# A two-block transformer kernel on one core: the tiles of SBUF laid out in another order, and the rows of x scaled before they are turned

## Time and profile before

| | |
|---|---|
| three runs, us | 1514.72, 1513.34, 1510.06; median 1513.34 |
| the profiled execution, us | 1509.91 |
| its span, first to last instruction, us | 1508.2 |
| PE busy | 1462.3 us (97%), 6907 matmuls |
| PE's weight loads busy | 1177.3 us (78%) |
| DVE, ACT, POOL busy | 789.5, 577.0, 102.6 us |

### The profile page before, as it was taken

One profiled execution on the slowest core, in us unless ns is written; L12 is line 12 of the kernel. 1 busy time (PEld: TensorE's weight loads), 2 busy tenths in 40 slices (PEclk: granted clock), 3 DMA queues, 4 the chain that ended last, 5 costly groups with the idle time before them and its releaser, 6 DMA issues.

```text
span 1508.2 us, 20254 instructions
## 1 busy us (share of the span) xinstructions
PE 1462.3 (97%) x6907; PEld 1177.3 (78%) x6907; DVE 789.5 (52%) x1232; ACT 577.0 (38%) x949; POOL 102.6 (7%) x83
## 2 busy tenths in 40 slices
PE   6999999899899999999999999999999999999997
PEld 5788877677867888888888777787787887878885
DVE  4538888775456544254445574344444344345552
ACT  5434444434545442124333353333333333333232
POOL 0000000101303000000033220000000000000001
PEclk9999999999999999999999999999999999999999
DMA  4322213223412333323323232221222312213231
GB/s 145 86 70 69 73 45 92 70 81 115 140 42 84 86 97 96 110 75 95 110 84 93 60 105 61 79 87 56 87 72 67 91 42 87 87 56 98 86 97 70
DMA packets 242783, 126.16 MB, mean 84 GB/s; under 512 B 17026, under 2 KB 241363, under 8 KB 242738
## 3 DMA queue, kind: packets, MB, share of 16 engines
q1 hardware_dynamic: 242162, 123.47, 28.3%
q10 hardware_dynamic: 576, 2.10, 0.4%
HBM read 123.45 MB, written 2.10 MB: 83 GB/s over the span
## 4 chain that ended last, share of the span: by engine, by line
PE 70%; issue 17%; DVE 4%; POOL 4%; ACT 2%; DMA 2%; SPq 0%; POOLq 0%; DVEq 0%; ACTq 0%
PE lin L556 20%; PE lin L560 19%; PE lin L559 19%; PE sc L633 3%; PE ob L647 3%; PE tr L641 1%; DVE wl L1394 1%; POOL kt L531 1%; ACT wh L1026 1%; POOL logit L538 1%; POOL qt L531 1%; PE tr L598 1%; PE sc L693 1%; DMA raw<-in_w_xkv_dram 1%; PE sc L598 1%
## 5 line engine op out<-in xcount | busy, mean ns | idle before, releaser
L1394 DVE TENSOR_TENSOR wl<-raw,wh 128x1024 fp32r<-128x1024 f32 x238 | 292.1, 1237 | 189.7 <-ACT wh L1026 185.2
L556 PE MATMUL lin<-uh,wh 128*128 128x512 f32 x752 | 304.2, 404 | 4.6 <-DVE pt L1867 2.0
L560 PE MATMUL lin<-uh,wl 128*128 128x512 f32 x752 | 294.1, 391 | 0.0
L559 PE MATMUL lin<-ul,wh 128*128 128x512 f32 x752 | 293.7, 390 | 0.0
L1026 ACT ACTIVATE wh<-raw 128x1024 fp32r<-128x1024 f32 x238 | 239.0, 1012 | 130.8 <-DMA raw<-in_w_mlp_dram 42.4
L556 PE MATMUL lin<-vh,wh 128*128 128x512 f32 x576 | 238.8, 415 | 1.7 <-DVE pt L1867 0.9
L559 PE MATMUL lin<-vl,wh 128*128 128x512 f32 x576 | 227.4, 395 | 0.0
L560 PE MATMUL lin<-vh,wl 128*128 128x512 f32 x576 | 227.3, 395 | 0.0
L556 PEld LDWEIGHTS lin<-uh,wh 128*128 128x128 f32 x752 | 141.7, 188 | 39.0 <-issue 4.6
L559 PEld LDWEIGHTS lin<-ul,wh 128*128 128x128 f32 x752 | 141.8, 189 | 29.8 <-issue 2.6
L560 PEld LDWEIGHTS lin<-uh,wl 128*128 128x128 f32 x752 | 141.5, 188 | 30.3
(11 more groups left out here) (356 smaller groups left out, 1721.1 us busy)
## 6 DMA issues: line engine op xcount, KB each, us to landing
raw<-in_w_in_dram SPq DMA_DIRECT2D x101, 512.0 KB, 3.6
raw<-in_w_mlp_dram SPq DMA_DIRECT2D x64, 512.0 KB, 4.0
raw<-in_w_out_dram SPq DMA_DIRECT2D x16, 512.0 KB, 3.5
raw<-in_w_xkv_dram SPq DMA_DIRECT2D x8, 512.0 KB, 3.5
raw<-in_w_proj_b_dram SPq DMA_DIRECT2D x8, 512.0 KB, 3.5
raw<-in_w_proj_a_dram SPq DMA_DIRECT2D x8, 512.0 KB, 3.5
xtok<-in_x_dram ACTq DMA_DIRECT2D x4, 512.0 KB, 5.1
raw<-in_w_mla_out_dram SPq DMA_DIRECT2D x4, 512.0 KB, 3.8
```

Source lines behind the costliest of these rows:

```text
L556: ins = pe.matmul(o, wh[:, slot, at], xh_, start=start, stop=False)
L559: pe.matmul(o, wh[:, slot, at], xl_, start=False, stop=False)
L560: return pe.matmul(o, wl[:, slot, at], xh_, start=False, stop=stop)
L1394: dve.tensor_tensor(wl[:, c.slot(4), 0:size], raw[:, c.slot(2), 0:size], wh[:, c.slot(4), 0:size].bitcast(F32), ALU.subtract).then_inc(lo_ ...
```

## The change

It has three parts. (1) The declarations of SBUF tiles are put in another order. From the bottom: `uh` 0 to 16 KB, `ul` 16 to 32; then the phase tiles, which share 32 to 96 KB: `vh` 32 to 48 and `vl` 48 to 64, `fh` 32 to 64 and `fl` 64 to 96, `cqh`, `cql`, `ckh`, `ckl` in 32 to 52, `yh`, `yl`, `oh`, `ol` in 32 to 64, `xuh`, `xul` in 32 to 64, `memh`, `meml` in 72 to 88, `xoh`, `xol` in 80 to 96, `gates`, `xtok`, `xn`, `av`, `gb` in 64 to 96; above them `wh` 96 to 112, `wl` 112 to 128, `raw` 128 to 136, `h` 136 to 152, then the tables and work tiles, `acc`, `ya` and the rest up to 207.3 KB. (2) A new tile `xn` holds x's rows times `rstd`. ACT takes the square root for each quarter by itself, that of quarter q - 1 behind the squares of quarter q; DVE takes its reciprocal and scales the 128x1024 quarter. PE waits for the four scaled quarters, and `turn_normed` is now a transpose, four of 128x128 for each tile. The diagonal tiles and `x_diag` go. (3) Two small DVE steps (`both`, `hb`) stand behind `lower(Idx(1))` in place of ahead of `norm_rstd("mix")`.

```diff
-        h = sb("h", [P, DT, S])
         uh = sb("uh", [P, DT, S], F32R)
         ul = sb("ul", [P, DT, S], F32R)
-        raw = sb("raw", [P, 2, 1024])
+
+        st = ExitStack()
+        cqh = sb("cqh", [P, 3, S], F32R, st)
...
+        st = ExitStack()
+        vh = sb("vh", [P, DT, S], F32R, st)
+        vl = sb("vl", [P, DT, S], F32R, st)
+        av = sb("av", [P, PAIRS, S], stack=st)
+        gb = sb("gb", [P, PAIRS, S], stack=st)
+        st.close()
+        fh = sb("fh", [P, 16, S], F32R)
+        fl = sb("fl", [P, 16, S], F32R)
         wh = sb("wh", [P, 4, 1024], F32R)
         wl = sb("wl", [P, 4, 1024], F32R)
+        raw = sb("raw", [P, 2, 1024])
+        h = sb("h", [P, DT, S])
...
@@ PE
-                for q in range(QT):
-                    ins = pe.matmul(sc[f % 3][:, q * P:(q + 1) * P], xtok[:, q, f * P:(f + 1) * P],
-                                    te[:, q * P:(q + 1) * P], start=True, stop=True)
-                ins.then_inc(xt_ready, 1)
+                turn_tile(sc[f % 3], lambda q: xn[:, q, f * P:(f + 1) * P]).then_inc(xt_ready, 1)
...
-            pe.wait_ge(x_diag, 1)
+            pe.wait_ge(xn_made, QT)
...
@@ ACT
+            def x_deviation(q):
+                act.wait_ge(xsq_made, q + 1)
+                act.activation(std[:, q:q + 1], x_sq[:, q:q + 1], ACT.Sqrt, bias=eps, scale=1.0 / D)\
+                    .then_inc(x_std if q < QT - 1 else std_made, 1)
+
             for q in range(QT):
                 act.wait_ge(x_landed[q], 16)
+                wait(act, xsq_made, q)
                 act.activation(logit[:, 0:D], xtok[:, q, :], ACT.Square, accum_out=x_sq[:, q:q + 1]).then_inc(xsq_made, 1)
-                act.wait_ge(xsq_made, q + 1)
-            act.activation(std, x_sq, ACT.Sqrt, bias=eps, scale=1.0 / D).then_inc(std_made, 1)
+                if q:
+                    x_deviation(q - 1)
+            x_deviation(QT - 1)
...
@@ DVE
+            def x_normed(q):
+                if q < QT - 1:
+                    dve.wait_ge(x_std, q + 1)
+                    dve.reciprocal(rstd[:, q:q + 1], std[:, q:q + 1]).then_inc(x_rstd, 1)
+                    dve.wait_ge(x_rstd, q + 1)
+                else:
...
+                dve.wait_ge(x_landed[q], 16)
+                dve.tensor_scalar(xn[:, q, :], xtok[:, q, :], rstd[:, q:q + 1], None, ALU.mult).then_inc(xn_made, 1)
+
+            x_normed(0)
+            x_normed(1)
             dve.wait_ge(vec_ready, 1)
             dve.tensor_copy(cols[:], tr[0][:, 0:NVEC]).then_inc(vec_copied, 1)
+            x_normed(2)
+            x_normed(3)
             dve.wait_ge(vec_copied, 1)
-            step(dve.tensor_tensor(both[:], cols[:, COL["final_norm_g"]:COL["final_norm_g"] + DT],
-                                   cols[:, COL["g_norm_2"]:COL["g_norm_2"] + DT], ALU.mult))
-            step(dve.tensor_scalar(hb, cols[:, COL["conv_ln_b"]:COL["conv_ln_b"] + CT], 0.5, None, ALU.mult))
-            norm_rstd("mix")
-            for q in range(QT):
-                ins = dve.tensor_scalar(te[:, q * P:(q + 1) * P], ident[:], rstd[:, q:q + 1], None, ALU.mult)
-            ins.then_inc(x_diag, 1)
             lower(Idx(0))
             for f in range(DT):
                 dve.wait_ge(xt_ready, f + 1)
                 gain_low(ul[:, f, :], sc[f % 3][:], col("norm_mix_g", f), uh[:, f, :], f + 1)
             lower(Idx(1))
+            step(dve.tensor_tensor(both[:], cols[:, COL["final_norm_g"]:COL["final_norm_g"] + DT],
+                                   cols[:, COL["g_norm_2"]:COL["g_norm_2"] + DT], ALU.mult))
+            step(dve.tensor_scalar(hb, cols[:, COL["conv_ln_b"]:COL["conv_ln_b"] + CT], 0.5, None, ALU.mult))
```

More of the change, by code:

```diff
@@ L164, in build @@
         ob = bank("ob")
-        h = sb("h", [P, DT, S])
         uh = sb("uh", [P, DT, S], F32R)
         ul = sb("ul", [P, DT, S], F32R)
-        raw = sb("raw", [P, 2, 1024])
+        st = ExitStack()
+        cqh = sb("cqh", [P, 3, S], F32R, st)
+        cql = sb("cql", [P, 3, S], F32R, st)
+        ckh = sb("ckh", [P, 2, S], F32R, st)
+        ckl = sb("ckl", [P, 2, S], F32R, st)
+        z = sb("z", [P, CT, S + PAD], stack=st)
+        st.close()
+        st = ExitStack()
+        yh = sb("yh", [P, CT, S], F32R, st)
+        yl = sb("yl", [P, CT, S], F32R, st)
+        oh = sb("oh", [P, 4, S], F32R, st)
+        ol = sb("ol", [P, 4, S], F32R, st)
+        s2 = ExitStack()
+        xtok = sb("xtok", [P, QT, D], stack=s2)
+        xn = sb("xn", [P, QT, D], stack=s2)
+        s2.close()
+        gates = sb("gates", [P, 16, S], stack=st)
+        st.close()
+        st = ExitStack()
+        xuh = sb("xuh", [P, DT, S], F32R, st)
+        xul = sb("xul", [P, DT, S], F32R, st)
+        s2 = ExitStack()
+        memtok = sb("memtok", [P, 2, D], stack=s2)
+        memh = sb("memh", [P, DT, MEM], F32R, s2)
+        meml = sb("meml", [P, DT, MEM], F32R, s2)
+        s2.close()
+        xp = sb("xp", [P, 2, QT, MEM], stack=st)
+        xpt = sb("xpt", [P, 2, 2, S], stack=st)
+        xoh = sb("xoh", [P, XH, S], F32R, st)
+        xol = sb("xol", [P, XH, S], F32R, st)
+        st.close()
+        st = ExitStack()
+        vh = sb("vh", [P, DT, S], F32R, st)
+        vl = sb("vl", [P, DT, S], F32R, st)
+        av = sb("av", [P, PAIRS, S], stack=st)
+        gb = sb("gb", [P, PAIRS, S], stack=st)
+        st.close()
+        fh = sb("fh", [P, 16, S], F32R)
+        fl = sb("fl", [P, 16, S], F32R)
         wh = sb("wh", [P, 4, 1024], F32R)
         wl = sb("wl", [P, 4, 1024], F32R)
+        raw = sb("raw", [P, 2, 1024])
+        h = sb("h", [P, DT, S])
         ident = sb("ident", [P, P])
@@ L204, in build @@
         st = ExitStack()
-        gates = sb("gates", [P, 16, S], stack=st)
         acc = sb("acc", [P, CT, S], stack=st)
         otok = sb("otok", [P, QT, S], stack=st)
[L208 to L218, removed]
         st.close()
         st = ExitStack()
-        xtok = sb("xtok", [P, QT, D], stack=st)
         vrows = sb("vrows", [P, P], stack=st)
@@ L226, in build @@
         xq = sb("xq", [P, XH, S], stack=st)
[L227 to L237, removed]
         xk = sb("xk", [P, XH, MEM], stack=st)
@@ L240, in build @@
         st.close()
[L241 to L250, removed]
-        ybh, ybl = uh, ul
[L252 to L256, removed]
+        ya = sb("ya", [P, PAIRS, S])
+        ybh, ybl = uh, ul
+        otp = sb("otp", [P, QT, P])
+        rbc = sb("rbc", [P, S])
+        nlog = sb("nlog", [P, S])
+        atok = sb("atok", [P, QT, P])
         cq = gates[:, 11:16, :]
@@ L274, in build @@
         x_landed = [sem(f"x{q}_landed") for q in range(QT)]
-        xsq_made, x_diag, x_turned = sem("xsq_made"), sem("x_diag_made"), sem("x_turned")
+        xsq_made, x_turned = sem("xsq_made"), sem("x_turned")
+        x_std, x_rstd, xn_made = sem("x_std"), sem("x_rstd"), sem("xn_made")
         raw_landed = [sem("raw0_landed"), sem("raw1_landed")]
@@ L1486, in _ @@
                     .then_inc(start_made, 1)
+            def x_normed(q):
[4 more added lines that the diff above has]
+                else:
+                    dve.wait_ge(std_made, 1)
+                    dve.reciprocal(rstd[:, q:q + 1], std[:, q:q + 1]).then_inc(rstd_made, 1)
+                    dve.wait_ge(rstd_made, 1)
+                dve.wait_ge(x_landed[q], 16)
+                dve.tensor_scalar(xn[:, q, :], xtok[:, q, :], rstd[:, q:q + 1], None, ALU.mult).then_inc(xn_made, 1)
+            x_normed(0)
+            x_normed(1)
             dve.wait_ge(vec_ready, 1)
             dve.tensor_copy(cols[:], tr[0][:, 0:NVEC]).then_inc(vec_copied, 1)
+            x_normed(2)
+            x_normed(3)
             dve.wait_ge(vec_copied, 1)
-            step(dve.tensor_tensor(both[:], cols[:, COL["final_norm_g"]:COL["final_norm_g"] + DT],
-                                   cols[:, COL["g_norm_2"]:COL["g_norm_2"] + DT], ALU.mult))
-            step(dve.tensor_scalar(hb, cols[:, COL["conv_ln_b"]:COL["conv_ln_b"] + CT], 0.5, None, ALU.mult))
-            norm_rstd("mix")
-            for q in range(QT):
-                ins = dve.tensor_scalar(te[:, q * P:(q + 1) * P], ident[:], rstd[:, q:q + 1], None, ALU.mult)
-            ins.then_inc(x_diag, 1)
             lower(Idx(0))
```

## The result

The changed kernel takes **1492.12 us** (median of 4 runs, 1489.7 to 1494.72) against 1514.03 for the kernel before (4 runs beside it, 1510.06 to 1514.94): ratio **0.986**, 95% interval 0.9839 to 0.9881. The forecast was 1491.1 us. The profiled execution took 1491.87 us, its span is 1490.1.

A forecast was written before the change was run, and what follows sets the result against it. PE bounds the kernel: matmul count times start-to-start distance. Gains of 19.0 us (layout) and 3.2 (start), with nothing for the moved DVE steps, took 1509.91 to 1487.7; plus 3.4 for the median gave 1491.1 us, range 1486 to 1500.

The forecast's parts named there:

- The stream of an fp32r tile is slower from a high address than from a low one: PE's 512-column matmuls: 226.7 ns from tiles at 16 to 48 KB, 233.3 from 119 KB up.
- the count of 3000 matmuls: 512-column matmuls whose streamed tiles leave the high part of SBUF; at 6.67 ns each, 20.0 us.
- The borders at 64 and 48 KB: Rivals on where fast SBUF places end: at 64 KB, 1493.4 us, chance 0.18; at 48 KB, 1500.0 us, chance 0.07.
- the third level under 16 KB: Rival: streamed tiles under 16 KB are faster still, 10.0 us more gain, 1481.1 us; chance 0.03.
- The place of the tile is not it: Rival: something else of the stages sets both paces, so only the start gains: 1510.1 us; chance 0.07.
- The weights' place counts as well: Rival: moving `wh`/`wl` up to 96 to 128 KB slows every job to 233.3 ns: 1525.1 us; chance 0.05.
- Pace, 19.0 us: Gain from moving every streamed tile under 96 KB, between 16.6 and 20.6 us.
- `pairs`: Stage taken as without idle time, so its whole matmul gain counts; expected near 464 us after.
- the 2.4 us counted: Part counted of the 3.4 us from 504 matmuls in stages that wait in places.
- Start, 3.2 us: First latent job's last matmul starts near 24.3 us instead of 27.55; bounds 1.5 and 4.0 us.
- the loss of 0.45 us: At the start, DVE's scaling of x's quarters ends about 12.9 us, where PE began at 12.48 before.
- the late rise at 19.4 us: Transposes don't lift PE's clock, so it rises at 19.4 us, not 16.8; start gains 1.9 us, total 1492.4.

The follow-up runs named there:

- experiment 3: Kernel after, with `wh`/`wl` at 32 to 64 KB and the streamed tiles of the stages at 64 to 128 KB: 1492.66 us, ratio 0.9872.
- experiment 6: Kernel after, with weights at 32 to 64 KB and `fh`/`fl` woven into one tile at 96 to 160 KB: 1492.1 us (one run).
- experiment 9: Kernel before, with only 224 unused bytes put between the tables and the tiles of the stages: 1497.67 us, ratio 0.9906.
- experiment 4: Kernel after, with `wh`/`wl` moved above everything, to 175 to 207 KB: 1520.56 us, ratio 1.0056.
- experiment 7: Kernel after, with 64 extra transposes breaking the second `down` stage ahead of every second k: mean matmul distance there 230.9 ns; no total given.
- experiment 8: Kernel before, with 64 extra transposes breaking the second `down` stage ahead of every second k: mean matmul distance there 231.6 ns; no total given.
- experiment 2: Kernel before, with the new order of declarations but the old start: 1500.01 us, ratio 0.9921.
- experiment 1: Kernel before, with the new start (x scaled into `xn`, turned by transposes) but the old places: 1507.8 us, ratio 0.9971.
- experiment 5: New start, with `uh`/`ul` at 0 to 32 KB, the stages' streamed tiles at 111 to 175, `wh`/`wl` at 175 to 207: 1503.17 us, ratio 0.993.
- experiment 10: Kernel after, padded so offsets from the weights are 32 bytes for `uh`/`ul`, 64 for stage tiles, 128 for `fh`/`fl`: 1515.51 us, ratio 1.0022.
- experiment 11: Kernel after, padded so offsets from the weights are 256 bytes for `uh`/`ul`, 384 for stage tiles, 448 for `fh`/`fl`: 1507.11 us, ratio 0.996.
- experiment 12: Kernel before, with 224 unused bytes, the new start, and the mem pair alone moved to offset 288: 1495.38 us, ratio 0.9877.

## Why the prediction was right, and where it was not

**The number was right and its reason wrong.** "The stream of an fp32r tile is slower from a high address than from a low one" is what failed. The two levels (226.7 and 233.3), the tiles that had them and the count of 3000 matmuls were read rightly, and the change brought all of them to 226.7 in unbroken stretches. But place and offset went together in the kernel before: its only streamed tiles at offset 0 were the two low ones. The mem pair, high like the rest, took 116.5 ns for 256 columns, which I read as half of 233.3, a loss that goes with the columns. That reading was wrong: after the change it took 120, so 256 columns lost nothing before. In the rows of before this could not be seen, but the addresses modulo a power of two were there to be worked out from the same declarations as the kilobytes.

**The rivals.** The borders at 64 and 48 KB had nothing behind them (experiments 3, 6 and 9), nor had the third level under 16 KB (`up1` took 87.04 us with `uh` there, 87.07 before). "The place of the tile is not it" had a chance of 0.07, and its premise is true; the step that didn't follow is "then only the start remains", since the new order also changed what does count. "The weights' place counts as well" was half right too: the weights' address decides together with the stream's (experiment 4), at 1520.6 us measured against 1525.1 worked out. It didn't come true in the change because `wh` went to 96 KB exactly, a multiple of 256 bytes like the streams.

**Pace, 19.0 us.** The unbroken stages gave what was forecast: 2.52, 2.56 and 1.28 in `down0`, `down1` and `proj_a`, against 2 x 2.56 and 1.28. **The term that was mis-sized is `pairs`**, taken as fully on the path at 6.67 ns for 1536 matmuls, 10.2 us (`pairs` near 464 us); it gave 5.8 (468.6 us). The step that failed is calling it a stage without idle time and stopping there: PE is busy for 467.0 of 468.6 us, but its fp32r stream is broken by other matmuls, and behind a break the good offset has not yet its pace (experiments 7 and 8). The trace of before could have shown it: on `uh`, fast as it was, the second to fourth distance behind a break averaged 232 ns. The other stages gave 2.1 of the 2.4 us counted, of which 1.2 came from the mem stage, whose share the prediction put at 0.6 at most, and not from pace: its matmuls became slower, and in experiment 2, with the same places, the stage gained only 0.1.

**Start, 3.2 us.** In the profiled run it was 3.65: 1.29 at the first product against 1.4 forecast, and 2.4 from five shorter cycles against 2.1. The scalings ended at 12.66, where 12.9 was expected, so the loss of 0.45 us was 0.33. Part of that gain is luck with the clock, as follows.

**The clock.** The first 12 transposes start 0.216 us apart in every run that turns by transposes, twice the 0.108 of later ones: the lower of the two levels. In the kernel after, the first product already goes at the upper level (0.31 and 0.23 us to the next), 2.9 us after PE began with nothing but transposes. In experiment 1, PE:

```profile
15.88 0.77 PE L558 MATMUL lin<-uh,wh 128*128 128x512 f32 x1
16.45 0.63 PE L561 MATMUL lin<-ul,wh 128*128 128x512 f32 x1
16.88 0.63 PE L562 MATMUL lin<-uh,wl 128*128 128x512 f32 x1
17.30 0.83 PE L600 MATMUL sc<-ident,xn 128*128 128x128 f32 x4
17.89 0.47 PE L558 MATMUL lin<-uh,wh 128*128 128x512 f32 x1
```

Distances of 0.57, 0.43 and 0.42 us are the lower level, until past 17.3. Experiments 3 to 6 and 10 look like this, and 7, 11 and 12 lie between (0.56, 0.27, 0.23 in experiment 12). Of the profiled runs with this start only that of the kernel after is at the upper level from its first product. The moment of the rise makes a difference of about a microsecond: the conv stage starts at 58.1 us in the kernel after, and between 58.5 (experiment 12) and 59.4 (experiment 3) in the six others with this start and `uh` at full pace. Against 61.8 before that is a gain of 2.4 to 3.3 us, where the prediction had 3.2. What sets the moment of the rise, these runs do not show. The Trainium skill (TensorE: Matmul & The Clock Gate, Part 4: PE-mode transpose) says that transposes don't count as activity that lifts the clock. The kernel after departs from that, since it rose behind transposes alone; none of the runs shows the late rise at 19.4 us that the prediction worked out for it; in every run the turning of tiles behind the second group of three products goes at 0.11 us a record.

**The sum.** 22.2 us against 18.0 between the profiled executions (1509.91 and 1491.87), so the sum was 4.2 too large, nearly all of it in `pairs`. The median came out only 1.0 us from the forecast because the other correction erred the other way: I put the median 3.4 us above the profiled execution, as before, and it lay 0.25 above. The hit is partly luck.

## What to carry to other kernels

For streams of 512 columns, give a streamed fp32r tile and the weight tile it meets addresses that are a multiple of 256 bytes apart, and put small tables of odd size above both or pad behind them; 224 unused bytes were worth 0.9% here. When two levels of a cost go with a property of a tile, list the tile's other properties (the address modulo a power of two, its distance to its partner) before one is given the credit, and move only one of them. A gain for each instruction, read in an unbroken stretch, has to be read again where other work breaks the stretch.

## What the runs showed of the hardware that was not expected

- TensorE's distance between dense fp32r matmuls of 512 columns depends on the addresses of its two operands in SBUF relative to each other: 226.7 ns at 0 and 226.8 at 256 bytes mod 512, 228.9 at 64, 233.3 at 32, 128, 224, 288, 384 and 448. Neither address alone matters (experiments 4 and 5). That its weight load and its stream get in each other's way is a guess that no run here shows directly.
- The Trainium skill (SBUF — State Buffer, SBUF: two separate sides) says that PE never waits on anyone there. No run contradicts that of other engines: the `down` stage took 87.04 us in six kernels with four orders of the tiles around it. But two operands of PE itself cost 2.9% by their distance.
- The Trainium skill (TensorE: Matmul & The Clock Gate, Back-to-back issue gap) gives about 131 ns as the sustained distance of load and matmul pairs of 512 columns, and about 216 ns as the isolated gap. The fastest dense pace here is 226.7; no run of this kernel comes near 131.
- After other matmuls the fp32r stream takes about ten matmuls to reach 226.7 ns (228.6 at the tenth distance in the kernel after); at an offset of 288 bytes it stays between 231.4 and 234.1 (before). Why it needs them stays open.
- With 256 columns the order is reversed: 119.7 ns on average at offset 0 (the kernel after, experiments 2 and 9), 117 at 288 (before, experiments 1 and 12) and 117.2 at 64 (experiment 10); 224 and 384 lie between, at 118.4 and 118.7 (experiments 4 and 11). Why stays open.
